# A two-layer streaming encoder on one core: TensorE's feed-forward steps put in a loop, and three orders of work changed

## The reference

```python
def trunk(x, ...):
    # layer 0: rmsnorm -> lru_mixer;  layer 1: rmsnorm -> rwkv7_mixer
    x = x + y
    hn = rmsnorm(x, norm_ffn[layer])
    y, fb = conv_ffn(hn, ffn_conv[layer], ...)
    x = x + y

def conv_ffn(h, buf, w_up, conv_w, conv_b, w_down):
    u, new_buf = causal_dwconv(h @ w_up, buf, conv_w, conv_b)   # width 3, per feature
    g, val = jnp.split(u, 2, axis=-1)
    return (jax.nn.gelu(g) * val) @ w_down, new_buf
```

## Time and profile before

| | |
|---|---|
| median of 3 | 3364.82 us |
| profiled execution | 3369.45 us, its span 3367.6 us |
| PE busy | 3053.2 us (91%) |
| DVE busy | 1665.9 us (49%) |
| ACT busy | 1156.3 us (34%) |
| POOL busy | 967.9 us (29%) |
| instructions fetched for PE (queue q8) | 254 packets, 4.16 MB |

### The profile page before, as it was taken

How to read it: one execution, slowest core, us unless ns; L and a number is a source line. 1 busy time by engine, 2 the same in 40 slices (tenths; PEclk the granted TensorE clock), 3 DMA queues, 4 the chain that set the end, 5 groups by cost and what they waited for, 6 DMA issues and landing times.

```text
span 3367.6 us, 73581 instructions
## 1 busy us (share of the span) xinstructions
PE 3053.2 (91%) x32214; PEld 2949.6 (88%) x32214; DVE 1665.9 (49%) x1691; ACT 1156.3 (34%) x1334; POOL 967.9 (29%) x521
## 2 busy tenths in 40 slices
PE   5999799999999998699968888886979999999996
PEld 5889689999999997699967777775979999999996
DVE  6555655454445456102216676774365454544455
ACT  4634322221222224433325666665132222212222
POOL 2222222222222224213313333443122222222221
PEclk9999899999999998799979999998989999999998
DMA  2111111111111110332222222212101111111111
GB/s 98 43 33 42 32 33 46 44 44 51 41 45 46 46 40 25 133 130 86 90 89 54 63 62 60 64 52 83 45 26 45 45 45 45 43 51 42 46 45 60
DMA packets 87562, 186.10 MB, mean 55 GB/s; under 512 B 28896, under 2 KB 51936, under 8 KB 87264
## 3 DMA queue, kind: packets, MB, share of 16 engines
q1 hardware_dynamic: 80352, 154.73, 14.9%
q10 hardware_dynamic: 6912, 26.84, 2.0%
HBM read 145.01 MB, written 36.53 MB: 54 GB/s over the span
## 4 chain that ended last, share of the span: by engine, by line
PE 79%; DVE 11%; ACT 4%; issue 2%; POOL 2%; DMA 1%; ACTq 0%; SPq 0%; DVEq 0%; POOLq 0%
PE PS L1113 68%; PE PS L1273 10%; DVE T L1548 2%; ACT T L464 2%; DVE T L1538 1%; DVE G L1538 1%; POOL HL L905 1%; DVE HL L1538 1%; DVE X L1538 1%; DVE M L1553 1%; PE PS L1226 1%; DVE NN L1538 1%; ACT L464 1%; PE PS L1145 1%; DVE HF L1548 1%
## 5 line engine op out<-in xcount | busy, mean ns | idle before, releaser
L905 POOL TENSOR_TENSOR WL<-RAW,WH 128x1024 fp32r<-128x1024 f32 x204 | 498.5, 2444 | 1513.5 <-ACT WH L464 1509.6
L1113 PE MATMUL PS<-HH,WH 128*128 128x364 f32 x3456 | 775.0, 333 | 76.5 <-POOL HL L905 42.9
L1113 PE MATMUL PS<-HH,WL 128*128 128x364 f32 x3456 | 771.0, 332 | 0.0
L1113 PE MATMUL PS<-HL,WH 128*128 128x364 f32 x3456 | 768.2, 331 | 0.0
L1113 PEld LDWEIGHTS PS<-HH,WH 128*128 128x128 f32 x3456 | 604.3, 190 | 89.6 <-issue 46.0
L1113 PEld LDWEIGHTS PS<-HH,WL 128*128 128x128 f32 x3456 | 609.2, 190 | 0.0
L1113 PEld LDWEIGHTS PS<-HL,WH 128*128 128x128 f32 x3456 | 606.8, 190 | 0.0
L1538 DVE TENSOR_TENSOR X<-PS,X 128x1092 f32<-128x1092 f32 x224 | 290.3, 1296 | 279.4 <-PE PS L1113 275.0
L1548 DVE SCALAR_TENSOR_TENSOR T<-T,FP 128x1092 f32<-128x1092 f32 x192 | 416.0, 2167 | 6.8
L464 ACT ACTIVATE WH<-RAW 128x1024 fp32r<-128x1024 f32 x204 | 216.5, 1061 | 367.2 <-PE PS L1113 344.8
L464 ACT ACTIVATE T<-PS 128x1092 f32<-128x1092 f32 (+1 forms) x125 | 135.4, 1083 | 600.6 <-PE PS L1113 580.7
(11 more groups left out here) (156 smaller groups left out, 3440.0 us busy)
## 6 DMA issues: line engine op xcount, KB each, us to landing
RAW<-weights SPq DMA_DIRECT2D x204, 512.0 KB, 3.6
scratch<-T ACTq DMA_DIRECT2D x32, 546.0 KB, 2.9
scratch<-SR ACTq DMA_DIRECT2D x16, 546.0 KB, 2.9
X<-xT SPq DMA_DIRECT2D x8, 546.0 KB, 8.5
yT<-T SPq DMA_DIRECT2D x8, 546.0 KB, 3.0
T<-scratch_m SPq DMA_DIRECT2D x8, 512.0 KB, 4.0
LW<-scratch SPq DMA_DIRECT2D x16, 192.0 KB, 2.6
KK<-scratch SPq DMA_DIRECT2D x16, 192.0 KB, 2.4
```

Of the source, the lines that this page charges most:

```text
L905: pool.tensor_tensor(out, full, hi, ALU.subtract).then_inc(*t.made(event))
L1113: mm = pe.matmul(acc[:, j, :], a, b[:, j * CW:(j + 1) * CW], start=(i == 0 and q == 0), stop=(i == len(blocks) - 1 and q == 2))
```

## The change

Four edits are made.

1. SP no longer waits for each of the five loads of an RWKV interval.
2. ACT does both `sh_hi` copies ahead of the norm's squares, where they stood ahead of the second and the fourth.
3. PE runs the ten middle feed-forward steps as a hardware loop of 5 turns over two steps, as the other engines do.
4. DVE's `conv` takes one down result, d0, ahead of its last SCALAR_TENSOR_TENSOR (before: d0 ahead of the first, d1 ahead of the last). d1 is taken ahead of `p_full`, d2 behind it.

```diff
-                        if job >= -1:
-
-                            sp.wait_ge(*t.at(f"dma_in{b}", t.n[f"dma_in{b}"]))
...
-            plus = added(m - KT)
-
-            def added_and_shift(k):
-                if k in (1, 3):
-                    act.wait_ge(*t.next("mu_w"))
-                    run(TR[:, 6 + k // 2, 0:D], T[:, k // 2, 0:D], ACT.Copy, "sh_hi")
-                plus(k)
-
-            norm(m, added_and_shift, n, "two")
+            for q in range(2):
+                act.wait_ge(*t.next("mu_w"))
+                run(TR[:, 6 + q, 0:D], T[:, q, 0:D], ACT.Copy, "sh_hi")
+            norm(m, added(m - KT), n, "two")
...
-                for s in range(1, STEPS - 1):
-                    m, n = step(m, n)
-                    m, n = down(m, n, s - 1)
+                with pe.Fori(0, FFN_TURNS) as turn:
+                    t.enter(turn, FFN_TURN)
+                    a, b = m, n
+                    for s in (1, 2):
+                        a, b = step(a, b)
+                        a, b = down(a, b, s - 1)
+                    t.leave(FFN_TURNS)
+                m, n = m + 24 * FFN_TURNS, n + 12 * FFN_TURNS
...
                 for j in range(last - 1, -1, -1):
+                    if j == 0 and between is not None:
+
+                        take(between, 0)
                     back = last - j
-                    if between is not None:
-                        take(between + back - 1, back - 1)
                     stt(out, src[:, PAD - back:ROW - back], taps[j], out, ALU.mult, ALU.add, "tap" if j else "conv")
...
                         if s and j:
-                            take(m + 2, 2)
+                            take(m + 1, 1)
...
-                        take_all(a, False, first=3)
+                        take_all(a, False, first=2)
```

More of the change, by code:

```diff
@@ L1742, in ffn @@
                 m = step(STEPS - 1, m)
-                take_all(m, False, first=3)
+                take_all(m, False, first=2)
                 m += KT
```

## The result

The changed kernel takes 3425.0 us (median of 4 executions, 3421.1 to 3430.8) against 3367.1 us for the kernel before on the same chip (3364.6 to 3372.1). The ratio is 1.0172, 95% interval 1.0151 to 1.0192: 57.9 us slower. The forecast was 3410 us, 45 us slower.

What follows compares the result with a forecast made beforehand. PE's unbroken feed-forward chains, half of the span, were taken as the bound. Takes 36, squares 4, loop 5 and SP's waits 0 us gave 3364.8 + 45 = 3410 us against the median, range 3388 to 3430.

Steps and rivals of the forecast that it cites:

- The bound: Both feed-forward layers: PE busy without a break, so whatever makes PE wait there is lost whole.
- The takes: Steps 1 to 11 of two layers: take(d0) behind an instruction held by POOL, d2 late 1.64 us, 22 places, 36.1 us.
- Rival A: Feed-forward steps: take(d0) ends by 600.84, so the takes don't stall PE; 3374 us, chance 0.08.
- The squares: One place, a layer's end: first square waits for the second copy, take(d3) 4.95 us late, 4 us after give-back.
- sums that run freer: Behind the late take(d3): POOL finishes its subtractions sooner, DVE's sums run freer, some delay comes back; 4 us taken.
- SP's waits: RWKV stage: loads have an interval of room, so landing earlier is worth 0, bounds -5 to +5.
- Rival C: RWKV stage: SP's chain of loads paced the intervals, which shorten; 3338 us at 3 us an interval, chance 0.04.
- The loop: PE's loop, 8 taken branches: code fetch mostly covered by queued matmuls, 0.6 us each, 5 us, bounds 0 to 39.
- Short gaps don't cost PE its clock: Takes term: from 135 to 220 us, PE idle for 5 us, the granted clock still has 0.98.
- The upper bound of 39 us: PE's loop: uncovered fetch at each of 8 taken branches, 4.9 us each from the worst rows for a small transfer.
- Rival B: PE's loop stalls: a return costs 4.0 us, 8 of them 32 us; 3437 us, chance 0.14.
- The predicted sign: Both feed-forward chains: the loop's part shows as PE idle time released by nothing (issue) every 144 us.

Runs made afterwards that it cites:

- Holding POOL back: The kernel with only the takes' order changed, plus POOL's second low part delayed until the fourth convolution is over: 3369.2 us, ratio 1.0015.
- putting the take back: The kernel with only the takes' order changed, but take(d0) again ahead of the first SCALAR_TENSOR_TENSOR, d1 and d2 still later: ratio 1.0004.
- slot 64: The kernel before plus PE's loop alone, with the loop's head placed at slot 64 in both layers: ratio 1.002.
- loop-alone kernel: The kernel before with only PE's hardware loop added, head not placed: 3394.6 us, ratio 1.009.
- slot 8 kernels: Two kernels with the loop's head at slot 8 in both layers: PE's loop alone, ratio 1.0004; the whole changed kernel, 3402.6 us, ratio 1.0105.
- 236: The kernel before plus PE's loop alone, with the loop's head placed at slot 236: 3387.6 us, ratio 1.0066.

## Why the prediction was right, and where its size was off

**The bound.** That PE's feed-forward chain loses in full whatever stalls it held: 1.62 us a place came out as 35 us of time. Within 0.2 us, the 23.0 us of layer 1 are 11 x 1.62 = 17.8 for the takes and 5.0 for the squares, and the 42.4 us of layer 2 are 17.8 for the takes and 25.9 for the loop, less 1.5 us of a shorter step ahead of the loop.

**The takes: 36.1 us predicted, 35 to 35.6 measured.** Each link was seen: the instruction begun beside POOL ended 1.16 us behind it, lasted 3.37 us, the take followed, d2 waited, d3 did not. Holding POOL back, and putting the take back, each removed the loss or nearly all of it. Rival A fell. The Trainium skill, page "SBUF — State Buffer", section "Who interferes with whom", has the exclusive hold that this shows. By the trace it is not quite whole: of the instruction's 1.36 us some 0.2 still fell beside POOL's span, as in the kernel before.

**The squares: 4 predicted, 5.0 measured.** The start was late by what was worked out: take(d3) 5.01 us late against 4.95, beside the 16.88 us by which this place had moved already. The 1 us that I took off for sums that run freer was not given back.

**SP's waits: 0 predicted, 0 measured** (interval -0.13 to +0.06%). Landing earlier changed nothing for the reader. Rival C fell. The RWKV stage was to keep its length to 5 us and came out 6.7 us shorter; kernels that keep SP's waits show the same length.

**The loop: 5 predicted, about 26 measured in the changed kernel.** This is the mis-sized term: 21 us more than given. The step read: each of the 8 returns fetches its target, at 1.6 + 1.06 + 1 us less 3.0 us of queue, 0.6 us. The runs show in its place:
- One fetch and its cover were sized about right: 3.4 to 3.9 us of branch, which starts 3.0 us ahead of the queued matmuls' end, and 1.0 to 1.1 us a return at slot 64.
- Whether anything is fetched hangs on where the head lies. Four returns (layer 1) cost nothing: by the count a body of 1755 instructions from slot 0 or 1 touches 7 blocks, and these stay.
- In layer 2 the head lies about two slots earlier, the body touches 8 blocks, and the return needs two fetches one behind the other. My sum had one fetch. The second has no cover: PE idles for 3.4 to 4.2 us.
- Behind seven of the eight such gaps PE ran at half clock for some groups, 0.91 us a group instead of 0.50; behind one of 3.44 us it didn't. "Short gaps don't cost PE its clock" held for the 1.7 us gaps (the group after has 0.61 us to the next one, then 0.50) and not for these.

In the loop-alone kernel the four returns cost 19.9 us, 5.0 each. In the changed kernel the turns of layer 2 last 762.3 us together against 736.3 with the head at slot 8: 25.9 us, 6.5 each, as six groups are slow instead of three or four. Why the slow piece is longer there was not settled. That the head's place is the cause, and not the jump, the waits or the register instructions, is shown by the slot 8 kernels, with the same instructions otherwise. That two fetches stand in series is shown by the times of the q8 packets. The slot of the plain loop's head is worked out from counts and from which layer fetched, and not read; the trace has three records ahead of the second wait where slot 254 leaves two, so it is good to a slot or so.

The upper bound of 39 us for eight returns, from "4.9 in the worst" row, rested on a misreading: the profile's transfers have a slower row, `PP<-pair_vec` with 2 KB each at 9.4 us.

Rival B had a return at 4.0 us, eight times. The mechanism came true at four of them, at a higher price, and its sum (32 us) is near the 26 for the wrong reason. The predicted sign, "issue" idle every 144 us in both layers, was right for neither: layer 1 had none, and layer 2's were put down to POOL.

The sum of the measured parts is 35.6 + 5.0 + 0 + 25.9 = 66.5 us. The two feed-forward layers show 65.4 of them; the stages at both ends and in the middle were 9.4 us shorter in this profile, which the runs of single parts show to be scatter for the middle. The medians give 57.9. From 3364.8 us the 66.5 would have led to 3431 us, just outside the range of 3388 to 3430. So it is in part luck that the time fell inside: the takes, the largest term, were right in mechanism and size, the loop was not.

## What to carry to other kernels

Before an instruction that a waiting engine needs soon is put behind a two-input DVE instruction, look whether a POOL instruction runs there: its end, and not the DVE duration, sets when the moved one is done. A large hardware loop on PE is free where its body touches few enough code blocks, and here cost 1 to 6.5 us a turn where the head lay some slots differently; count the body, compare q8 between two places with the same code, and set the head's slot. A releaser named behind a gap is a guess: where the same code elsewhere has no such gap, ask what else differs.

## What the runs showed of the hardware

- PE's loop body of 1755 instructions from slot 8 ran five turns with branches of 0.2 to 0.3 us and no idle piece (no q8 packet in 540 us in layer 1 of the changed kernel, branch 0.21 to 0.25 us). With 8 blocks all of them were fetched again, 32 packets in a stretch of 540 us, 9 a return, branch 3.3 to 4.1 us. 7 blocks are kept and 8 are not.
- A return's price by the slot of the head, this body: 8: 0; 64: 1.0 to 1.1 us; 236: 2.2 to 2.7 us; about 254: 5.0 us, and 6.5 in the changed kernel.
- The Trainium skill, page "Runtime: NRT & Kernel Launch", section "Instruction fetch mechanics", says that there is no instruction cache to gain from and that a taken branch to code outside the current window of two pages stalls. The stall is seen here; a jump back over 7 kept blocks without one differs from it, and the measurement decides. The same section gives PE's instruction memory room for 2048 instructions, which is 8 blocks, and has the next page fetched while one runs. With one block for that, 7 kept blocks fit it; this is a reading that no run here tests.
- Behind gaps of PE of 3.4 to 4.2 us seven of eight returns had 2.7 to 5.5 us at 0.91 us a group, the lower of its two levels (granted clock 0.82 over the 19.5 us shown); behind gaps of 1.7 us there was none.
